# Hybrid decoder layer: another tile order, the convolution's steps moved, and a bank copied in one instruction

## The reference

```
h = rms_norm(x, norm_w);  proj = h @ w_in
q, kv, gates, nsa_z, cv_h, cv_b, cv_c, cv_z = split(proj)
o_nsa  = (g0 * o_cmp + g1 * o_slc + g2 * o_win) * silu(nsa_z)   # 8 heads of 64: three attention branches
u      = cv_c * cv_h
o_conv = cv_b * (causal conv, width 3, of u, + conv_b) * silu(cv_z)   # 512 channels
out    = x + concat(o_nsa, o_conv) @ w_out
```

## Time and profile before

| | |
|---|---|
| median of 3 runs | 678.46 us (677.49 to 678.79) |
| the profiled execution | 678.36 us, of it 676.6 us span |
| TensorE busy | 654.6 us, 97% |
| VectorE / ScalarE / GpSimd busy | 484.9 / 379.5 / 197.0 us |
| granted TensorE clock | 1.000 |

### The profile page before, as it was taken

How to read it: one execution, slowest core, us unless ns; L and a number is a source line. 1 busy time by engine, 2 the same in 40 slices (tenths; PEclk the granted TensorE clock), 3 DMA queues, 4 the chain that set the end, 5 groups by cost and what they waited for, 6 DMA issues and landing times.

```text
span 676.6 us, 10300 instructions
## 1 busy us (share of the span) xinstructions
PE 654.6 (97%) x3513; PEld 550.9 (81%) x3513; DVE 484.9 (72%) x1151; ACT 379.5 (56%) x883; POOL 197.0 (29%) x216
## 2 busy tenths in 40 slices
PE   8999999999999999999989999899899999999998
PEld 5889998878887888888777888788678788887776
DVE  4945989984756555776687876878877768777753
ACT  6744458554435354466555674657875556655641
POOL 3423204523423232431222312123842221212120
PEclk9999999999999999999999999999999999999999
DMA  8423202211111111100101101011411001001111
GB/s 316 140 55 111 63 1 63 63 32 47 50 45 32 47 32 32 48 18 30 32 16 32 32 17 31 1 63 55 162 35 60 34 32 63 32 32 38 57 32 63
DMA packets 19636, 36.30 MB, mean 54 GB/s; under 512 B 2816, under 2 KB 4224, under 8 KB 19584
## 3 DMA queue, kind: packets, MB, share of 16 engines
q1 hardware_dynamic: 19440, 35.63, 16.9%
q10 hardware_dynamic: 144, 0.00, 0.0%
HBM read 31.43 MB, written 4.19 MB: 53 GB/s over the span
## 4 chain that ended last, share of the span: by engine, by line
PE 81%; DVE 10%; ACT 4%; issue 4%; DMA 1%; SPq 0%; POOL 0%; ACTq 0%; DVEq 0%
PE pf L1398 10%; PE pf L1399 9%; PE pf L1400 9%; PE tp L1691 7%; PE sc L1536 4%; PE pj L1400 4%; PE pj L1399 4%; PE pj L1398 4%; PE sc L1535 4%; PE po L1671 4%; PE po L1672 4%; PE sc L1398 3%; PE sc L1400 3%; PE sc L1399 3%; DVE ptl L1332 1%
## 5 line engine op out<-in xcount | busy, mean ns | idle before, releaser
L904 ACT CAST pth<-tp 128x512 fp32r<-128x512 f32 (+1 forms) x148 | 86.8, 586 | 119.8 <-PE tp L1691 118.6
L1310 DVE CUSTOM_DVE_ANT_0 sc<-sc,maskb 128x64 f32<-128x64 f32 (+8 forms) x192 | 103.2, 561 | 49.9 <-PE sc L1536 49.3
L1332 DVE TENSOR_TENSOR ptl<-tp,pth 128x512 fp32r<-128x512 f32 x132 | 91.1, 690 | 39.1 <-ACT pth L904 38.5
L627 POOL TENSOR_SCALAR qp<-qp,precip,gate 128x64 f32<-128x64 f32 x64 | 44.4, 694 | 175.4 <-DVE precip L1300 175.2
L1691 PE MATMUL tp<-cst,qp 128*128 128x128 f32 (+1 forms) x592 | 88.9, 272 | 2.4 <-issue 1.3
L1398 PE MATMUL pf<-hh,fh 128*128 128x512 f32 x200 | 80.6, 403 | 2.7 <-DVE mixc L1269 1.9
L1691 PEld LDWEIGHTS tp<-cst,qp 128*128 128x128 f32 (+1 forms) x592 | 68.8, 137 | 12.3 <-issue 3.4
L1399 PE MATMUL pf<-hl,fh 128*128 128x512 f32 x200 | 78.3, 392 | 0.0
L1400 PE MATMUL pf<-hh,fl 128*128 128x512 f32 x200 | 78.2, 391 | 0.0
L587 POOL TENSOR_TENSOR fl<-fraw,fh 128x512 fp32r<-128x512 f32 x36 | 48.7, 1354 | 92.7 <-ACT fh L753 92.7
L578 POOL TENSOR_TENSOR wl<-qp,wh 128x512 fp32r<-128x512 f32 (+1 forms) x33 | 49.3, 1519 | 88.8 <-ACT wh L667 85.2
(11 more groups left out here) (243 smaller groups left out, 1548.5 us busy)
## 6 DMA issues: line engine op xcount, KB each, us to landing
fraw<-in_wside SPq DMA_DIRECT2D x36, 256.0 KB, 2.6
qp<-in_wpack SPq DMA_DIRECT2D x28, 256.0 KB, 3.1
wor<-in_wout SPq DMA_DIRECT2D x16, 256.0 KB, 2.8
xo<-in_x SPq DMA_DIRECT2D x16, 256.0 KB, 2.8
out<-xo SPq DMA_DIRECT2D x16, 256.0 KB, 2.1
mixc<-in_xcm SPq DMA_DIRECT2D x4, 512.0 KB, 7.2
xlow<-in_xcm SPq DMA_DIRECT2D x3, 512.0 KB, 6.4
qp<-in_wpack SPq DMA_DIRECT2D x5, 224.0 KB, 2.6
```

What stands on the lines that cost most here:

```text
L904: nc.scalar.copy(pth[ptn % 2][0:r, :], tp[tpn % 2][0:r, :]).then_inc(pth_ready, 1)
L1310: return V.tensor_tensor_reduce(row, row, mask, -1.0, -NEG, ALU.add, ALU.min, most)
L1332: V.tensor_tensor(ptl[ptn % 2][:, :], tp[tpn % 2][:, :], pth[ptn % 2][:, :].bitcast(F32), ALU.subtract).then_inc(tp_read, 1)
```

## The change

1. TILES: the order in each t becomes ch, cc, cz, cb. The wait for the finished convolution moves from cb to the second product of cz; cb waits for cz. The last tile of all is thus cb, with no tanh.
2. ScalarE's third tap (L877) leaves the side half and becomes `convolve_first`, in the step after, behind the exponentials and the first transposed tile.
3. VectorE's first piece of the convolution moves to the end of its step, the others behind the side half of the first group.
4. A unit's output: ScalarE copies the whole bank `po` to a new tile `oc` in one 128x512 instruction, and VectorE adds each half of `po` to the other half of `oc`.
5. Before the main loop both engines take the first two keys before z1 and z2, VectorE also before it normalises the compressed key.

```
-    TILES += [("ch", t, 1816 + P * t), ("cc", t, 2840 + P * t), ("cb", t, 2328 + P * t), ("cz", t, 3352 + P * t)]
+    TILES += [("ch", t, 1816 + P * t), ("cc", t, 2840 + P * t), ("cz", t, 3352 + P * t), ("cb", t, 2328 + P * t)]
...
             root(S_CK, 1, HD, ck_std)
+            keys_hi(0, 4, 1)
             item(E_Z, 1)
             item(E_Z, 2)
-            keys_hi(0, 4, 1)
...
-                elif kind == "cc" and f % 2 == 1:
-                    bank_free(act, f - 1)
-                    bank_free(act, f)
-                    A(mixc[:, t, :], ub[:, 2:2 + SEQ], ACT.Identity, ...).then_inc(conv_first, 1)
+            def convolve_first(t):
+                f = 2 * CONV_TILES[t] + 1
+                bank_free(act, f - 1)
+                bank_free(act, f)
+                A(mixc[:, t, :], ub[:, 2:2 + SEQ], ACT.Identity, ...).then_inc(conv_first, 1)
...
                 for kind, _ in turned[:1]:
                     prob_hi(kind)
+                if k - 1 in CONV_STEPS:
+                    convolve_first(CONV_STEPS.index(k - 1))
...
-                    nc.scalar.copy(ot[0:HD, :, :], o4[HD:P, :, 0, :])
-                    nc.scalar.copy(ot[HD:P, :, :], o4[0:HD, :, 1, :]).then_inc(ot_copied, 1)
+                    nc.scalar.copy(oc[:, :], po[:, :]).then_inc(ot_copied, 1)
...
             V.tensor_reduce(stat[:, 0, S_CK:S_CK + 1], cksq[:, :], AX.X, ALU.add).then_inc(ck_sum, 1)
+            keys_lo(0, 4, 1)
             inv_std(S_CK, 1, HD, ck_std, 1)
...
                 elif kind == "cb":
                     dve.wait_ge(f_done, f + 1)
-                    if f % 2:
-                        dve.wait_ge(conv_done, t + 1)
+                    dve.wait_ge(cz_used, 2 * t + f % 2 + 1)
                     V.tensor_tensor(mc, side_bank(f), mc, ALU.mult).then_inc(f_free[bank_of(f)], 1)
...
                     bank_free(dve, f)
-                    V.scalar_tensor_tensor(mc, th[:, :], 0.5, mc, ALU.mult, ALU.mult).then_inc(cz_done, 1)
+                    if f % 2:
+                        dve.wait_ge(conv_done, t + 1)
+                    V.scalar_tensor_tensor(mc, th[:, :], 0.5, mc, ALU.mult, ALU.mult).then_inc(cz_used, 1)
...
-                    V.tensor_tensor(ot[0:HD, :, :], o4[0:HD, :, 0, :], ot[0:HD, :, :], ALU.add)
-                    V.tensor_tensor(ot[HD:P, :, :], o4[HD:P, :, 1, :], ot[HD:P, :, :], ALU.add).then_inc(o_read, 1)
+                    c4 = oc[:, :].rearrange("p (a b q) -> p a b q", a=2, b=2)
+                    V.tensor_tensor(ot[0:HD, :, :], o4[0:HD, :, 0, :], c4[HD:P, :, 0, :], ALU.add)
+                    V.tensor_tensor(ot[HD:P, :, :], o4[HD:P, :, 1, :], c4[0:HD, :, 1, :], ALU.add).then_inc(o_read, 1)
                 if 1 <= k <= NS:
                     scale(k - 1)
-                for t, j in conv_pieces_at(k):
-                    convolve(t, j)
                 for f in side_ends(k, 0):
                     if f < NF:
                         side(f)
                 for c in out_ends(k, 0):
                     residual(c)
+                for t, j in conv_pieces_at(k):
+                    if j:
+                        convolve(t, j)
...
                 for c in out_ends(k, 1):
                     residual(c)
+                for t, j in conv_pieces_at(k):
+                    if j == 0:
+                        convolve(t, j)
```

More of the change, by code:

```diff
@@ L229, in mixn_half_at @@
     return None
-CONV_STEPS = [step_of(16 * n + 15) for n in range(NTILES) if TILES[n][0] == "cc"]
+CONV_TILES = [n for n in range(NTILES) if TILES[n][0] == "cc"]
+CONV_STEPS = [step_of(16 * n + 15) for n in CONV_TILES]
 def conv_pieces_at(k):
@@ L241 @@
     for hf in range(2):
-        assert step_of(16 * TILES.index(("cb", t, 2328 + P * t)) + 8 * hf + 7) >= c + 2 + 2 * hf
+        assert step_of(16 * TILES.index(("cz", t, 3352 + P * t)) + 8 * hf + 7) >= c + 2 + 2 * hf
 WOUT_STEP = step_of(OUT_0 - 9) + 1
@@ L347, in hybrid_layer @@
                 th = sb("th", [P, 512], F32, d)
+                oc = sb("oc", [P, 512], F32, d)
                 with ExitStack() as f:
@@ L390, in hybrid_layer @@
         fh_ready, fl_ready, half_used = sem("fh_ready"), sem("fl_ready"), sem("half_used")
-        f_done, f_tanh, cz_done = sem("f_done"), sem("f_tanh"), sem("cz_done")
+        f_done, f_tanh, cz_used = sem("f_done"), sem("f_tanh"), sem("cz_used")
         f_free = [sem(f"f_free{s}") for s in range(2)]
@@ L866, in side @@
                     if kind == "cz" and 2 * t + f % 2:
-                        act.wait_ge(cz_done, 2 * t + f % 2)
+                        act.wait_ge(cz_used, 2 * t + f % 2)
                     if kind == "z" and f >= 1:
@@ L873, in side @@
                     nc.scalar.copy(mixc[:, t, cols], side_bank(f)).then_inc(f_free[bank_of(f)], 1)
-                elif kind == "cc" and f % 2 == 1:
-                    bank_free(act, f - 1)
-                    bank_free(act, f)
-                    A(mixc[:, t, :], ub[:, 2:2 + SEQ], ACT.Identity, scale=prm[:, P_CW + 3 * t + 2:P_CW + 3 * t + 3],
-                      bias=prm[:, P_CB + t:P_CB + t + 1]).then_inc(conv_first, 1)
+            def convolve_first(t):
+                f = 2 * CONV_TILES[t] + 1
+                bank_free(act, f - 1)
+                bank_free(act, f)
+                A(mixc[:, t, :], ub[:, 2:2 + SEQ], ACT.Identity, scale=prm[:, P_CW + 3 * t + 2:P_CW + 3 * t + 3],
+                  bias=prm[:, P_CB + t:P_CB + t + 1]).then_inc(conv_first, 1)
             def exponentials(s):
@@ L959, in _ @@
                     if m == 0:
-                        act.wait_ge(f_done, NF)
-                        act.wait_ge(cz_done, 8)
+                        bank_free(act, NF - 1)
                     else:
@@ L1227, in _ @@
             item(E_Z, 2)
-            keys_lo(0, 4, 1)
             hidden(1)
```

1 line of the change is left out of this document (removed).

## The result

The changed kernel takes 670.42 us (median of 4 runs, 670.26 to 670.84) where the kernel before, beside it, takes 678.1 (677.49 to 678.79). The ratio is 0.9887, with a 95% interval of 0.987 to 0.9905: 7.7 us less. The forecast was 672.9, 5.5 us less, in a range from 670.8. The direction was right, the gain was larger than forecast, and the time lies just under the range.

The account below looks back on a forecast made before the run. TensorE, busy 97% of the span, was taken as the bound, with only its 22 us idle to win. Gains less a 0.8 us loss summed to 5.55 us: 678.4 - 5.5 = 672.9 us, range 670.8 to 676.5.

Parts of the forecast that it names:

- What bounds the kernel, and the third tap: TensorE 97% busy, only 22 us idle to win; tap behind queued work gains 1.1 (steps 14, 30), 1.29 (51), 1.46 (75).
- Keys before the loop: Before the main loop: 1.4 us won at the third key transpose, about 0.6 given back at first side matmul; gain 0.8.
- cz where cb was: Steps 53 and 77: the product that frees the side bank starts earlier; gain 0.75 us each, 0.2 to 0.4 wait left.
- The loss in step 81: A low part comes behind cz's tanh and two products of step 80: loss 0.8 us, bounds 0 and 1.4.
- The output copy: One 128x512 copy instead of two, 0.14 us less on ScalarE 16 times, crossing free; gain 0.2 us in all.
- Steps 86 to 88: Long wait of 1.42 us ends ScalarE's chain from the queries' copy; earlier VectorE work only lengthens it; gain 0.
- the sum: Gains and the step 80 loss over all places, added from idle times: 5.55 us, giving 672.9 us.
- more than forecast: Rival: idle records understate TensorE's loss at waits, and step 80's loss is absent; some 7.5 us, 670.9; chance 0.12.
- The later part of the loop: Sign of a wrong prediction: the later half, where only the output copy changed, moves by over 0.5 us.
- Given back on VectorE: Rival: moved scalings and pieces meet GpSimd three times, costing 2.4 us: 675.3; sign: more scalings over 1.2 us; chance 0.25.
- Waits that only change place: Rival: ScalarE and VectorE set the rate, so removed waits return in the next steps; 677.6 us; chance 0.10.
- The crosswise add: Rival: 32 adds across halves at half speed cost VectorE 13.8 us, TensorE 6.9; 679.8 us; chance 0.05.

## Why the prediction was right, and where it was short

**What bounds the kernel, and the third tap: right.** The idle time of TensorE was all there was to win, and the tap ahead of queued work was the main cause: 6.4 us came with the tap and the pieces.

**Keys before the loop: right** in both halves, +1.55 and -0.76 for +1.4 and -0.6. The part measured alone gives the same.

**cz where cb was: the size right, the heading wrong.** The working named the piece of the convolution that no longer stands ahead of the product, and that was the cause: 0.75 and 0.70. But it stood under the swap of tiles. With the pieces moved and the tiles not, the gains came, and with the tiles swapped alone they didn't. The waits left there, 0.32 and 0.23, are within the 0.2 to 0.4 forecast. The loss in step 81 was forecast at 0.8 and was 0.92 (wait 0.69).

**The output copy: short.** 0.59 for the copy, right, and no price for crossing, right. Where 0.2 us was forecast the part alone shows 0.7, most of it at three waits, in a trace; its interval can't confirm it.

**Steps 86 to 88: 0 was forecast, -0.5 measured.** The wait became longer, 1.42 to 1.88, as said. What wasn't foreseen is the clock behind it: at the two waits alone the order gave 0.47 and lost 0.46.

**The step that failed is the sum: terms too small, and places priced at nothing.** The sum took idle times from brackets, and a bracket understates a wait. A matmul's record lasts 0.39 us where its successor starts 0.23 after it, so the first 0.16 us of a wait behind such a matmul show no idle time. For each of the waits that were removed the ledger gives more than its bracket: 1.55 for 1.38, 1.01 for 0.82, 0.54 for 0.28, 1.48 for 1.29, 1.57 for 1.46. That is 0.9 us over five waits. And where little more than that is lost, no bracket is printed. TensorE's timeline of the kernel before shows how such a place looks:

```profile
337.73 0.39 PE L1399 MATMUL pf<-hl,fh 128*128 128x512 f32 x1
337.96 0.39 PE L1400 MATMUL pf<-hh,fl 128*128 128x512 f32 x1
338.40 0.41 PE L1535 MATMUL sc<-kst,qh 128*128 128x384 f32 x1
```

From 337.73 the next starts after 0.23, from 337.96 after 0.44, and no wait is printed. Six such places gave 1.63 us, two took 0.34, and two later ones gave 0.32. The sum had 0.2 for all of them, as the price of the output copy.

The largest share of the six, 0.92, comes from the order of tiles. The prediction said of steps 83 and 86 that cb is cheaper there by a tanh and a product and put "Gain 0", for the long wait of step 87; it had no term for step 59. In both places a low part had stood behind the second product of cz. So it was in the kernel before, in two rows of VectorE and one of TensorE:

```profile
369.24 0.69 DVE L1275 SCALAR_TENSOR_TENSOR mixc<-th,mixc 128x512 f32<-128x512 f32 x1
...
370.64 0.68 DVE L1332 TENSOR_TENSOR ptl<-tp,pth 128x512 fp32r<-128x512 f32 x1
...
371.38 0.50 PE L1671 MATMUL po<-pth,val 128*128 128x512 f32 x1
```

So 0.9 at five waits and 1.4 at these places beyond their 0.2, less 0.3 at three terms that came out a little worse, are the 2.0 between 5.55 and 7.5. That the 0.51 at the first loads and the -0.51 of steps 86 to 88 cancel is luck. The prediction had the bracket as half of its rival "more than forecast", with 670.9 and a chance of 0.12; the median is 0.5 below even that. The other half of that rival, no loss in step 80, did not happen, so its figure lies near for partly wrong reasons. The sum should have taken some 0.16 more for each wait, and a look at the starts instead of the brackets.

The later part of the loop, where only the output copy changed, moved by 0.32, within the 0.5 that was set as a bound for the working.

The 0.51 at the first loads is no part of the change. The kernel before waited 1.3 us there for `hh` in its profiled run, and other kernels, none of which changes that part, waited up to 1.2. From the waits of TensorE, first the changed kernel, then the one with cz's product moved, whose only edit takes effect 430 us later:

```profile
PE xt L1442 <- ACT hh L680: 0.2, 1, 0.2
```

and

```profile
PE xt L1453 <- ACT hh L680: 1.1, 1, 1.1
```

**The rivals.** Given back on VectorE: it didn't happen. The scalings' mean went from 623 to 614 ns and their longest from 1.42 to 1.43 us, and of the 96 six took over 1.2 us before and three after; the prediction's sign for this rival was that they become more. Each that took over 0.9 us, eight before and seven after, lies over a subtraction of GpSimd; in each trace 21 scalings of 640 columns had only GpSimd's own scaling beside them and took 0.61 to 0.62, as those with nothing beside them. The rule of the port pair from the Trainium skill ("SBUF — State Buffer", Who interferes with whom) was not tested by itself; one row agrees with it, the scaling that took 1.34 us beside GpSimd and 0.55 in its new place, alone. Waits that only change place: not for the tap; it is what the two kernels with all the casts and the copy moved showed. The crosswise add: refuted, 0.42 to 0.43 as before.

## What to carry to other kernels

When an instruction waits on a late input, look at what is queued behind it on its engine: ScalarE stood idle for some 2 us ahead of each tap with exponentials or a transposed tile ready behind it, and putting the tap behind them gave 5 us without removing any work. Price a wait of TensorE from start to start of its matmuls, not by the idle time printed, and hold two kernels' n-th matmuls against each other to see where a lead comes and goes. Before moving work from an engine that is late, look for the engine that feeds on it: the casts moved with the copy cost 3.0 us (670.49 to 673.46), and moved without it, from step 86 on, they gave 2.1 (to 668.34; 1.8 by the ratios).

## What the runs showed of the hardware

**TensorE's clock fell to half behind a standstill.** Granted clock of the changed kernel by stretch (start:end, length, busy time of PE, PEld, DVE, ACT, POOL, then the clock, DMA share, GB/s):

```profile
466.00:469.00 3.00, 1.10 (x6) 0.69 (x6) 1.68 (x6) 3.00 (x9) 2.05 (x2) 1.00 0.66 231
469.00:470.00 1.00, 0.87 (x3) 0.90 (x4) 0.51 (x1) 1.00 (x3) 1.00 (x2) 0.51 0.63 223
470.00:471.00 1.00, 1.00 (x6) 0.91 (x5) 0.96 (x4) 1.00 (x4) 1.00 (x2) 0.50 0.49 170
471.00:472.00 1.00, 1.00 (x5) 0.91 (x4) 0.97 (x3) 0.94 (x3) 1.00 (x2) 0.50 0.36 131
472.00:474.00 2.00, 2.00 (x12) 1.64 (x11) 1.70 (x3) 0.56 (x2) 2.00 (x3) 0.89 0.20 53
```

TensorE had stood for 0.43 and 1.88 us, and then ran for over 3 us at 1.2 instead of 2.4 GHz, with matmuls of 512 columns 0.43 us apart instead of 0.23. Eight of fourteen profiled kernels show such a stretch before TensorE's last matmul, each only one. It begins between 0.1 us before and 1.2 us after the end of a wait of TensorE, between 468 and 479 us. It moved with the wait: in the kernel with casts and copy moved it stands behind the 2.31 us that ended at 475.83, and none stands where the wait of step 87 had been.

```profile
468.00:469.00 1.00, 1.00 (x7) 0.54 (x5) 0.96 (x3) 1.00 (x4) 0.89 (x1) 1.00 0.27 102
...
476.00:477.00 1.00, 1.00 (x6) 0.90 (x6) 0.00 (x0) 0.50 (x2) 0.00 (x0) 0.68 0.57 156
477.00:478.00 1.00, 1.00 (x4) 0.71 (x3) 0.85 (x3) 1.00 (x3) 0.32 (x1) 0.50 0.31 119
```

Where the waits of step 86 and 87 were shortened (0.44 and 0.83; 0.89 and 0.38; 0.44 and 1.35) the clock stayed at 1.00. Length alone does not decide it: the kernel before had 0.89 and 1.42 us and kept 1.00, the tap and the pieces together had 0.88 and 1.43 and fell to 0.50. Nor does the kernel alone: of the 47 runs of the kernel before beside the experiments, 12 show a mean granted clock of 0.997, as the profiled runs with one such stretch do, and its profiled run shows 1.000. What else decides stays open. That the wait of step 87 has a part in it is borne out by the two kernels with step 86 left without casts: none of their 15 runs is under 0.999. The expectation that one cast moved would keep the clock at 1.00 held in the profiled run, with more standing still around it (1.94 us, 3.4 us later), but another of its four runs has 0.995.

The cost is smaller than the stretch looks. In the kernel with cz's product moved it stretched the matmuls by 1.5 us in all, of which 0.9 came back, since the next wait for VectorE was then covered. Of the changed kernel's four runs the two with a granted clock of 0.997 took 670.84 and 670.5 us, the two with 1.0 took 670.26 and 670.34: about 0.4 us. Of 25 runs of the kernel before, the six with 0.997 have a mean of 678.97 us and the other 19 one of 678.10: 0.9 us.
